# Moving four modulation pieces from the output projection into the row projections of a two-layer mixer and expert block

## The reference

```python
h = h + hybrid_mixer(rms_norm(h, norm1_g[layer]), w_in[layer], ...)
h = h + expert_choice_ffn(rms_norm(h, norm2_g[layer]), w_router[layer], ...)
```

```python
def ada_mods(cond, w, b):
    m = (jax.nn.silu(cond) @ w + b)[..., None, :]
    return jnp.split(m, N_MOD, axis=-1)
```

## Time and profile before

| | us |
|---|---|
| median of 3 runs | 1953.57 |
| lowest and highest | 1952.56 and 1953.98 |
| the profiled execution, its own time | 1954.41 |
| its span in the profile | 1952.6 |
| TensorE busy | 1696.5 (87%) |
| VectorE busy | 791.1 (41%) |
| ScalarE busy | 526.9 (27%) |
| read from HBM | 622.01 MB, 320 GB/s over the span |

### The profile page before, as it was taken

The page is one execution under the profiler, slowest core; times in us unless marked ns, Lnnn a source line. Parts: engine busy times, 40 slices in busy tenths (PEclk is TensorE's granted clock), DMA queues, the critical chain, the costliest instruction groups (busy, mean ns, idle before and its releaser), DMA issues.

```text
span 1952.6 us, 26219 instructions
## 1 busy us (share of the span) xinstructions
PE 1696.5 (87%) x10892; PEld 1125.2 (58%) x10892; DVE 791.1 (41%) x1203; ACT 526.9 (27%) x802; POOL 30.0 (2%) x27
## 2 busy tenths in 40 slices
PE   7999877689888679998868887977789999999998
PEld 6877433245344249776343543522279985448897
DVE  6595312101111044975101111120077676647776
ACT  5633222100000037342100000021164343444342
POOL 0000000000000000000000000000030000000000
PEclk9999889889989989998989989979799999999999
DMA  9478999999999995679999999999955464315451
GB/s 358 162 269 335 425 430 421 427 422 423 420 427 421 426 385 182 242 265 419 427 423 423 423 424 421 426 428 423 416 190 196 172 233 154 129 49 208 175 182 55
DMA packets 125511, 626.57 MB, mean 321 GB/s; under 512 B 5091, under 2 KB 7779, under 8 KB 100198
## 3 DMA queue, kind: packets, MB, share of 16 engines
q1 hardware_dynamic: 124978, 624.85, 79.5%
q10 hardware_dynamic: 436, 0.32, 0.1%
HBM read 622.01 MB, written 3.15 MB: 320 GB/s over the span
## 4 chain that ended last, share of the span: by engine, by line
PE 58%; DMA 32%; ACT 4%; DVE 4%; issue 1%; SPq 0%; POOL 0%; DVEq 0%; ACTq 0%
DMA ring<-in_w_up 15%; PE bank L567 9%; PE bank L569 9%; PE bank L568 9%; DMA ring<-in_w_mlp_in 8%; DMA ring<-in_w_mlp_out 6%; PE bank L1086 6%; PE bank L1104 5%; PE bank L947 5%; PE bank L1332 2%; PE bank L580 2%; PE bank L1449 1%; DMA ring<-in_w_down 1%; PE bank L982 1%; PE bank L723 1%; DMA ring<-in_w_ada 1%
## 5 line engine op out<-in xcount | busy, mean ns | idle before, releaser
L947 PE MATMUL bank<-ring,xeT 128*32 128x512 f32 x1920 | 266.4, 702 | 98.2 <-DMA ring<-in_w_up 97.8
L947 PEld LDWEIGHTS bank<-ring,xeT 128*32 128x32 f32 x1920 | 68.6, 121 | 283.5 <-issue 283.0
L475 ACT ACTIVATE silu_g<-bank 128x256 f32<-128x256 f32 x32 | 12.3, 383 | 690.1 <-PE bank L947 690.1
L475 DVE TENSOR_TENSOR hid_e<-silu_g,bank 128x256 f32<-128x256 f32 x32 | 13.5, 421 | 374.0 <-ACT silu_g L475 374.0
L2567 DVE TENSOR_TENSOR w_low<-ring,w_high 128x1024 fp32r<-128x1024 f32 x128 | 152.4, 1233 | 10.2 <-ACT w_high L1858 5.3
L1858 ACT ACTIVATE w_high<-ring 128x1024 fp32r<-128x1024 f32 x128 | 126.5, 1050 | 85.0 <-PE bank L569 85.0
L1086 PE MATMUL bank<-ctx_xT,ring 128*128 128x256 f32 x512 | 125.3, 410 | 26.1 <-DMA ring<-in_w_mlp_in 26.1
L567 PE MATMUL bank<-x_high,w_high 128*128 128x256 f32 x512 | 145.1, 283 | 3.0 <-DVE x_low L475 2.4
L982 PE MATMUL bank<-ring,hid_T 128*32 128x256 f32 x1920 | 120.5, 397 | 30.9 <-DMA ring<-in_w_down 23.6
L568 PE MATMUL bank<-x_low,w_high 128*128 128x256 f32 x512 | 144.8, 283 | 0.0
L569 PE MATMUL bank<-x_high,w_low 128*128 128x256 f32 x512 | 144.7, 283 | 0.0
(11 more groups left out here) (282 smaller groups left out, 2595.9 us busy)
## 6 DMA issues: line engine op xcount, KB each, us to landing
ring<-in_w_down SPq DMA_DIRECT2D x60, 2048.0 KB, 30.2
ring<-in_w_up SPq DMA_DIRECT2D x60, 2048.0 KB, 24.3
ring<-in_w_gate SPq DMA_DIRECT2D x60, 2048.0 KB, 21.8
ring<-in_w_ada SPq DMA_DIRECT2D x24, 2048.0 KB, 9.6
ring<-in_w_mlp_in SPq DMA_DIRECT2D x24, 2048.0 KB, 8.4
ring<-in_w_mlp_out SPq DMA_DIRECT2D x24, 2048.0 KB, 7.9
ring<-in_w_in SPq DMA_DIRECT2D x16, 2048.0 KB, 9.2
ring<-in_w_out SPq DMA_DIRECT2D x4, 2048.0 KB, 7.8
```

The costliest lines, as they stand in the source:

```text
L475: self.ins, self.mine = op(*args, **kw), "none"
L947: ins = mm(ps[32 * j:32 * j + 32, :], xeT[:, g % 2, c, i * CAP:(i + 1) * CAP], w[:, :, k, j, :, :], start=c == 0, stop=c == KC - 1, skip_g ...
```

## The change

Two more pieces of each layer follow the row projections, so that each of the eight halves has one; two pieces of each layer are left over, in the two places at the router, and none is in the output projection. `ADA_REST` has two pieces per layer instead of four; which columns of `w_ada` a layer works on as a whole stays the same. ScalarE's copies move with the pieces, and so do the slots: both pieces of the router are loaded after the first expert weights, as before.

```diff
-EARLY_AFTER = ((RV, 0), (RV, 1), (HI, 1), (RG, 0), (HG, 0), (HG, 1))
+EARLY_AFTER = tuple((kind, t) for kind in (RV, HI, RG, HG) for t in range(2))
...
-ADA_EARLY = (pieces(0, 0, 6), pieces(0, 10, 12) + pieces(1, 0, 4))
-ADA_REST = (pieces(0, 6, 10), pieces(1, 4, 6) + pieces(1, 10, 12))
+ADA_EARLY = (pieces(0, 0, 8), pieces(0, 10, 12) + pieces(1, 0, 6))
+ADA_REST = (pieces(0, 8, 10), pieces(1, 10, 12))
...
             if (kind, 1) in EARLY_AFTER:
                 item(("ada", *next(early)), d, 1)
-        for piece, slot in zip(ADA_REST[layer], (b, d)):
-            item(("ada", *piece), slot, 1)
         rounded = [4 + (SPLITS * layer + j) % 2 for j in (OUT_0, OUT_1)]
...
-        for piece, slot in zip(ADA_REST[layer][2:], (b, d)):
+        for piece, slot in zip(ADA_REST[layer], (b, d)):
             item(("ada", *piece), slot, 1)
...
             turn_mixed(1, lambda t: freed(pe, ("hgrn_o", l, t)))
-            rest_ada(0)
             rows_times(take(pe, names[1], 1), 1, out_0, None, chunks=first)
             fill(rows_times(psum[0], 0, out_0, 1, chunks=second), names[0])
-            rest_columns(0)
-            rest_ada(1)
             fill_and_release(rows_times(psum[1], 1, out_0, None, chunks=second), names[1],
                              ("w_out", l, 0))
-            rest_columns(1)
...
             turn_rows(1)
-            rest_ada(2)
+            rest_ada(0)
             logits(1)
-            rest_columns(2)
+            rest_columns(0)
...
-            rest_ada(3)
-            rest_columns(3)
+            rest_ada(1)
+            rest_columns(1)
...
             high_item(l, OUT_1)
             high_chunks(("mix", l), mix_gain, (2, 3))
-            for k in range(2):
-                ada_row(ADA_REST[l][k])
...
-                     + [("ada", *piece) for piece in ADA_EARLY[l] + ADA_REST[l][0:2]])
+                     + [("ada", *piece) for piece in ADA_EARLY[l]])
...
-                        for piece in ADA_REST[l][2:]:
+                        for piece in ADA_REST[l]:
```

More of the change, by code:

```diff
@@ L1685, in _ @@
             step(f(spare[:, :], eps[:, :], ACT.Exp))
-            ada_row(ADA_REST[l][2])
+            ada_row(ADA_REST[l][0])
             for t in range(NT):
@@ L1692, in _ @@
                        bias=rstats[:, t, 1:2], accum_out=rstats[:, t, 2:3]), name)
-            ada_row(ADA_REST[l][3])
+            ada_row(ADA_REST[l][1])
             def ctx_stats(src):
```

## The result

The changed kernel took 1978.82 us (median of 4 runs, 1975.62 to 1979.73) beside 1953.28 us for the kernel before (4 runs): ratio 1.0123, 95% interval 1.011 to 1.0135. It is slower, as forecast, but by 25.5 us and not by 14.6, and outside the range. The profiled execution took 1979.73 us, span 1977.9.

What follows compares the result with a forecast made beforehand. The prediction took the expert-load stream, which starts late in the mixer, as the bound: 11.3 us moved work plus 5.9 waits less 2.6 given back is +14.6, giving 1968.2 us, range 1961.5 to 1972.5 us.

Steps and rivals of the forecast that it cites:

- What bounds the kernel: TensorE bounds the row projections, the full stream of expert loads the expert stages; work ahead of the stream's start is paid.
- C: Rival: TensorE sets the expert stage's end too, so moved work cancels up to 4.4 us; +8.4, 1962.0 us; chance 0.08.
- D: Rival: VectorE paces the row projections, so pieces there cost nothing; 1944.8 us, or 1951.0 if the stream bounds; chance 0.05.
- an expert stage that ends less late than it starts: Expert stages: a sign named in advance that would show the forecast wrong.
- The first expert only 4 us later: Start of the expert stage: expected sign, first expert 4 us later than before, the last about 7 us later.
- The moved work: Row projections: two pieces per layer moved ahead of the stream's start, 5.66 us of TensorE per layer, 11.3 in all.
- The new waits: Row projections, pieces of HI 0, RG 0, HG 0: late loads add 2.7 us in layer 0, 3.2 in layer 1.
- rival B: Row projections: the new loads are hidden after all, no added waits; +8.7 us, 1962.3 us; chance 0.07.
- What the stream gets back: First expert load: it lands sooner on an empty queue, 1.3 us back per layer, at most 2.1 and 1.5.
- The output projection at 0: Output projection: losing two pieces (5.66 us of TensorE) gains nothing, since it is hidden under the stream.
- about 1 us: w_out's second column half: forecast length of TensorE's new wait for VectorE.
- the 25 us of loads: Output projection: five loads free to go at once, 10.5 MB at 427 GB/s, keep the stream fed meanwhile.

Runs made afterwards that it cites:

- e5: The kernel before, with the matmuls of the first two early pieces per layer done three times, ahead of the first expert load: 1968.98 us, ratio 1.0071.
- e8: The changed kernel with 96 throwaway matmuls per layer put in the output projection where the two pieces were: 1974.11 us, ratio 1.009.
- e10: The changed kernel unaltered, timed again in a second session: 1975.20 us, ratio 1.011.
- e4: The kernel before, with the matmuls of the two pieces inside each output projection done three times, behind the first expert load: 1961.39 us, ratio 1.003.
- e7: The changed kernel with the loads of the six waiting pieces cut to 1 MB each (wrong modulation, same TensorE work): 1958.16 us, ratio 1.0013.
- e3: The kernel before, with the load of w_out's first half issued just behind the next piece's load in each layer: 1948.57 us, ratio 0.9965.
- e6: The changed kernel with 32 throwaway matmuls ahead of the load wait at the pieces of HI 0, RG 0 and HG 0: 1970.45 us, ratio 1.0081.
- e9: The changed kernel with 32 throwaway matmuls behind the load wait, just ahead of the pieces of HI 0, RG 0, HG 0: 1979.36 us, ratio 1.0131.
- e1: The changed kernel with the loads of HG's weight and both w_out halves issued just behind the next piece's load: 1963.27 us, ratio 1.0039.

## Why the prediction came out as it did

**What bounds the kernel: right.** Share 1.01 to the last expert; 13.6 us paid for work ahead of the stream's start (e5), nothing told for 5.7 us per layer behind it (e8 beside e10). Rivals C and D are out: C by e4 beside e5 (which alone would fit C too) and by e8, D by e5 and because the pieces moved the start in full. One sign of being wrong was badly chosen: "an expert stage that ends less late than it starts". The forecast's own sum has that (8.3 us late at the start, 7.1 at the end), and so has the measurement (15.55 and 12.3), for reasons that leave the bound as it is. "The first expert only 4 us later" was in truth 11.4 us, since the start itself was so much later.

**The moved work, 11.3 us: right.** e7 isolates it. At the start of the stream (T0 and T1) layer 0 shows +5.0 us, the later start of its row projections taken off, and layer 1 +4.0 (878.01 - 713.43 against 871.52 - 710.93); 5.66 - 1.2 + 0.5 = 5.0 and 5.66 - 1.64 = 4.0 were due.

**The new waits, 2.7 and 3.2 us: right places, too small.** Measured more were 5.57 - 1.22 = 4.4 and 6.76 - 1.64 = 5.1 us. The first step that failed took the landing of a load behind a weight from three rows of the kernel before (9.5, 9.7, 9.9 us), and bounded one wait by the worst that was seen there, 1.64 us. The six landings now lie at and above the end of that range. A wait is a small difference of two large numbers (10.3 - 8.3): landings 6% longer made the waits 40% longer. The bound had to be wider than two waits seen. The rule of rival B goes the other way. The Trainium skill, DMA: Bandwidth & Descriptors, section Anatomy of one DMA, gives some 2.0 us fixed plus bytes over 436 GB/s, an estimate of 6.8 us for a lone 2 MB, and gives it for loads that GpSimd issues, which the prediction does not say. SyncE issues the loads here; the rows show 7.6 to 8.1 us alone and up to 11.1 behind others, and the measurement decides.

**The clock: missing from the sum.** This is the step that failed by most. The forecast costed a wait at its own length and had no term for what the clock does at it. Of the shortfall it is the largest term: 4.8 us in layer 0 and 4.4 in layer 1, 9.2 in all, in the profile after; 6.8 in e10. In the row projections the kernel before gave no warning, since the clock stood at 1.00 behind 1.22 and 1.64 us. But its trace had the price of a piece at half clock, in the router of both layers, behind thin products and waits of under 0.9 us:

```profile
209.07 3.64 PE L580 MATMUL bank<-ring,silu_c 128*32 128x512 f32 x16
...
912.57 3.64 PE L580 MATMUL bank<-ring,silu_c 128*32 128x512 f32 x16
```

That is 1.7 us more than the 1.92 of the row projections, with a granted clock of 0.50 (912.57 to 916.20 us). The Trainium skill, TensorE: Matmul & The Clock Gate, Part 1: The HAM clock gate, says that the clock is set by how busy the engine has been recently. The trace agrees in that all 15 drops in the row projections of the twelve profiles stand at waits for a piece. The forecast needed a rival that prices each of the six waits with a piece at half clock (1.7 us, 10.3 in all from these rows); it had none.

**What the stream gets back, 1.3 us per layer: too small.** The landings gained 2.0 and 1.9 us, about the upper bound in layer 0 and above it in layer 1 (2.1 and 1.5), and all of it reached the end: from the stream's start to the landing of the last `w_up` (the rows of the chain above) it is 2.1 and 1.8 us less. The stage from start to end gained 3.3 us (542.88 to 539.62) and 2.0 (546.17 to 544.15). The rest of layer 0 is the clock once more, at the last expert's product of `w_up`, in the kernel before and after:

```profile
692.59 6.58 PE L947 MATMUL bank<-ring,xeT 128*32 128x512 f32 x32 [3.42 <-DMA ring<-in_w_up]
...
706.02 5.45 PE L941 MATMUL bank<-ring,xeT 128*32 128x512 f32 x32 [4.27 <-DMA ring<-in_w_up]
```

The same 32 matmuls take 6.58 and 5.45 us, with a clock of 0.69 and 0.82 around them. In layer 1 they take 6.45 and 6.22. The eight profiles of the changed kernel and its variants have 5.1 to 5.5 us in layer 0 and 5.1 to 6.5 in layer 1. What sets the clock there is not shown and no part of the forecast covered it: that it gave back 1.4 us is luck.

**The output projection at 0: right,** with the wait of 0.89 us where "about 1 us" was written. The reason given was too generous: the cover is about 4 us (e4), not the 25 us of loads that were counted. Moving more work into this place would have been costed wrongly.

The sum with the measured terms: 11.3 moved, 9.5 more waiting, 9.2 of clock, 0.8 because the row projections of layer 0 started later in this profile (not so in e10), less 3.9 by the stream and 1.4 by the last experts' products, is 25.5 us; the ends of the expert stages show 25.5. Of the 10.9 us by which the forecast fell short, the clock is 9.2, the waits are 3.6, the later start is 0.8, and stream and last experts take 2.7 off.

## What to carry to other kernels

Where a stage lives off a full stream of transfers, find the instruction that starts the stream: work ahead of it is paid in full, work behind it is free only until the next slot that the stream needs, so follow the slots until the cover is used up. When loads have to land within a step of fixed length, compare their landings over the whole trace with it, take the worst and more, and try the order of the issues first: here the turn of one load (e3) removed all waits for pieces from the kernel before. Price a new wait of TensorE with a stretch at half clock as well as its own length; a trace can show that price in another stage, as the router did here. If the wait can't be removed, put idle matmuls ahead of it (e6).

## What the runs showed of the hardware

- **A wait of TensorE can cost its length again.** Each short drop of the clock to 0.50 withheld 1.7 us; it fell between 1.2 us before the wait's end and 1.3 us behind it, and what it withheld from the waiting engine itself cost nothing. Of the waits for pieces in the row projections, all seven above 2.1 us (in the changed kernel, e10, e8 and e9) had a drop, and none of 1.10 us or less had. Between, runs differ: one at 1.19 (e1), 1.52, 1.61, 1.62, 1.69, 1.70, 1.82 and 1.90, none at 1.12, 1.15, 1.16, 1.22, 1.50, 1.60, 1.61, 1.62, 1.64, 1.65, 1.70, 1.71, 1.76 and 1.89. TensorE's wait of 1.85 or 1.86 us for VectorE just ahead of the row projections (80.69 us in the kernel before) had none in any of the 24 layers. And in the router the clock was at 0.50 with waits of under 0.9 us. What besides the length decides is open.
- **Loads of 2 MB in one queue:** 7.6 to 8.1 us alone in the row projections of both kernels; 7.6 to 9.1 for a weight issued 5.7 us behind a piece; 9.5 to 11.1 for a piece issued 4.5 us behind a weight (9.9 to 10.9 in e10). The same place can differ by over a microsecond between two executions of one kernel (issued near 864 us: 11.1 and 9.9).
- **The changed kernel varies by session** (1978.82 and 1975.20 us) where the kernel before stays within 2.1 us (medians 1953.28 to 1955.40): waits at the edge of a landing and the drops at them add up differently.
